# Expert pairs with many tokens: TensorE's code moved behind the program, and a way for up to 64 tokens

## The reference

```python
def hier_moe(x, rg_w, rg_b, re_w, re_b, w_gu, w_down):      # 32 experts, 2 of them per token
    g_p, g_idx = lax.top_k(softmax(t @ rg_w + rg_b), 1)     # one of 4 groups
    e_p, e_idx = lax.top_k(softmax(e_logits), 2)            # two of its 8 experts
    gate = g_p * e_p / sum(e_p)
    ...
    hg, hu = jnp.split(xb @ w_gu[e], 2, axis=-1)            # w_gu: 1024 x 1024 per expert, f32
    y = (jax.nn.silu(hg) * hu) @ w_down[e]                  # w_down: 512 x 1024
    out[token] += gate * y
```

## Time and profile before

| | |
|---|---|
| runs | 2184.54, 2185.58, 2190.74 us; median 2185.58 |
| profiled execution | 2183.85 us, its span 2182.0 us |
| mean granted TensorE clock | 0.92 |
| TensorE matmul busy | 1792.8 us, 82% of the span, 13574 rows |
| VectorE, ScalarE busy | 598.6 us, 394.0 us |
| read from HBM | 535.28 MB |
| instruction queue q8 | 173 packets, 2.83 MB |
| chain that ended last | PE 68%, DMA 19%, issue 5%, DVE 4%, ACT 3% |

### The profile page before, as it was taken

How to read it: one execution, slowest core, us unless ns; L and a number is a source line. 1 busy time by engine, 2 the same in 40 slices (tenths; PEclk the granted TensorE clock), 3 DMA queues, 4 the chain that set the end, 5 groups by cost and what they waited for, 6 DMA issues and landing times.

```text
span 2182.0 us, 30973 instructions
## 1 busy us (share of the span) xinstructions
PE 1792.8 (82%) x13574; PEld 1121.4 (51%) x13574; DVE 598.6 (27%) x1032; ACT 394.0 (18%) x761; POOL 36.0 (2%) x28
## 2 busy tenths in 40 slices
PE   6999999999999987776676778799987677876654
PEld 4788884879886764322222233565984322322211
DVE  1133312123421145321111121574345221211112
ACT  2323201313301133100000001151222000100001
POOL 0000000000000000000000000001030000000000
PEclk9999999999999998888878999899998788988886
DMA  8322333333243523899999998123004899999995
GB/s 336 99 92 97 135 135 142 146 78 130 83 155 135 212 112 129 369 424 425 424 425 425 426 402 318 66 77 117 4 23 182 375 424 425 418 425 425 426 424 225
DMA packets 51468, 539.56 MB, mean 247 GB/s; under 512 B 7441, under 2 KB 16273, under 8 KB 18225
## 3 DMA queue, kind: packets, MB, share of 16 engines
q1 hardware_dynamic: 49248, 527.06, 59.2%
q0 software_dynamic: 1152, 6.29, 0.8%
q10 hardware_dynamic: 848, 3.00, 0.4%
HBM read 535.28 MB, written 1.05 MB: 246 GB/s over the span
## 4 chain that ended last, share of the span: by engine, by line
PE 68%; DMA 19%; issue 5%; DVE 4%; ACT 3%; DVEq 0%; ACTq 0%
PE ps L410 53%; PE ps L417 13%; DMA arena<-in_moe_w_gu 7%; DMA arena<-in_moe_w_down 7%; DMA ring<-in_moe_w_down 3%; PE ps L423 3%; DMA ring<-in_moe_w_gu 1%; DVE x L1371 1%; ACT arena L2172 1%; DVE arena L1360 1%; ACT hb L2168 1%; DVE mT L1947 0%; ACT arena L2443 0%; DVE mT L1950 0%; ACT L2168 0%
## 5 line engine op out<-in xcount | busy, mean ns | idle before, releaser
L410 PE MATMUL ps<-hT,ring 128*128 128x256 f32 (+2 forms) x1888 | 392.0, 372 | 0.0
L410 PEld LDWEIGHTS ps<-hT,ring 128*128 128x128 f32 (+2 forms) x1888 | 330.5, 184 | 53.8 <-issue 3.4
L417 PE MATMUL ps<-arena 128*32 128x512 f32 (+1 forms) x1572 | 243.5, 706 | 107.5 <-issue 68.1
L417 PE MATMUL ps<-ring,arena 128*32 128x512 f32 x1472 | 211.0, 707 | 99.3 <-issue 73.3
L2172 ACT ACTIVATE arena<-ps 128x512 f32<-128x512 f32 (+4 forms) x145 | 94.5, 652 | 888.5 <-PE ps L417 519.8
L410 PE MATMUL ps<-arena 64*64 64x64 f32 (+10 forms) x1944 | 186.6, 324 | 58.8 <-ACT arena L2443 22.2
L417 PEld LDWEIGHTS ps<-arena 128*32 128x32 f32 (+1 forms) x1572 | 63.9, 130 | 264.0 <-issue 204.8
L1360 DVE TENSOR_TENSOR arena<-arena,ps 128x256 f32<-128x256 f32 (+2 forms) x82 | 46.0, 561 | 551.2 <-ACT arena L2168 464.2
L410 PEld LDWEIGHTS ps<-arena 64*64 64x64 f32 (+4 forms) x1944 | 113.2, 159 | 132.5 <-issue 54.0
L417 PEld LDWEIGHTS ps<-ring,arena 128*32 128x32 f32 x1472 | 53.7, 125 | 238.4 <-issue 196.2
L410 PE MATMUL ps<-ring,hT 128*128 128x256 f32 (+4 forms) x576 | 150.1, 419 | 8.7 <-ACT hT L2168 7.0
(11 more groups left out here) (174 smaller groups left out, 1258.8 us busy)
## 6 DMA issues: line engine op xcount, KB each, us to landing
ring<-in_moe_w_gu SPq DMA_DIRECT2D x64, 2048.0 KB, 27.7
arena<-in_moe_w_gu SPq DMA_DIRECT2D x64, 2048.0 KB, 30.9
arena<-in_moe_w_down SPq DMA_DIRECT2D x32, 2048.0 KB, 32.1
ring<-in_moe_w_down SPq DMA_DIRECT2D x32, 2048.0 KB, 31.8
ring<-in_w_merge SPq DMA_DIRECT2D x16, 2048.0 KB, 7.3
ring<-in_w_in SPq DMA_DIRECT2D x10, 2048.0 KB, 7.5
ring<-in_attn_w_qkv SPq DMA_DIRECT2D x6, 2048.0 KB, 7.4
ring<-in_rw_w_rkv SPq DMA_DIRECT2D x6, 2048.0 KB, 7.4
```

Source lines behind the costliest of these rows:

```text
L410: i = t.matmul(o, l, r, start=first, stop=last, skip_group_check=True)
L417: i = t.matmul(o, l, r, start=first, stop=last, skip_group_check=True)
```

## The change

Three things are done.

First, in TensorE's program each pair now has only the common way in place, right behind a compare-and-branch. The rare ways of all 32 pairs are written at the very end of the program, behind the last stage (`rare`, called through `rest`). A pair that goes a rare way branches there and, at its end, branches back to the place behind its common way (`over`). At the beginning of each rare way an instruction (BRANCH_PREFETCH_HINT) announces the branch at its end.

Second, there is a new way with two rounds for 33 to 64 tokens, names with `m2`; that with three is now `m3`. The functions `several(pr, before, R)` write both on all three engines. In the two-round way the gather has 64 columns instead of 128 per row.

Third, a flag `flag3` (over 64 tokens) is worked out by two more VectorE operations and loaded on the rare ways. On VectorE and ScalarE the code stays in place: within the branch for over 32 tokens and not over 96 there is one branch more, with the three-round way first.

The parts of the diff that count (moved code left out):

```diff
@@ tensor_program, moe
+        def several(pr, before, R):
...
+            t.wait_ge(*dve(N + W + "places"))
+            t.wait_ge(*act(N + "all in"))
+            w2 = 2 * CAP * (R - 1)
+            for half in range(2):
+                mm([(psum[1][:, k * P:k * P + w2], x[:, i, k * P:(k + 1) * P], e.oh2[:, i * P:i * P + w2], i == 0, i == 1)
+                    for k in range(4 * half, 4 * half + 4) for i in range(NT)], N + W + f"tokens{half}")
...
+        def rare(pr, before, origin):
+
+            N = M + f"{pr} "
+            with t.bass.body(N + "rare", parent=origin, valid_engines=[t.engine]):
+                more = t.value_load(e.flag3[0:1, pr:pr + 1], min_val=0, max_val=1)
+                t.br_ne(more, 0, N + "more", N + "two")
+                with t.bass.body(N + "two", valid_engines=[t.engine]):
+                    back = t.mark_branch_hint_location()
+                    several(pr, before, 2)
+                    t.br(N + "over").branch_hint(back)
+                with t.bass.body(N + "more", valid_engines=[t.engine]):
+                    most = t.value_load(e.flag2[0:1, pr:pr + 1], min_val=0, max_val=1)
+                    t.br_ne(most, 0, N + "any", N + "three")
+                    with t.bass.body(N + "three", valid_engines=[t.engine]):
+                        back = t.mark_branch_hint_location()
+                        several(pr, before, 3)
+                        t.br(N + "over").branch_hint(back)
...
-            many = t.value_load(e.flag[0:1, pr:pr + 1], min_val=0, max_val=1)
-            with t.If(many != 0):
-                most = t.value_load(e.flag2[0:1, pr:pr + 1], min_val=0, max_val=1)
-                with t.If(most != 0):
...
+            starts.append((pe.n, t.bass.cur_bb))
...
+            t.br_ne(many, 0, N + "rare", N + "common")
+            with t.bass.body(N + "common", valid_engines=[t.engine]):
+                up_to_cap(pr, pe.n)
+                t.br(N + "over")
+            t.bass.switch_bb(N + "over")
...
+        def rest():
+            end = pe.n
+            for pr, (before, origin) in enumerate(starts):
+                rare(pr, before, origin)
+            pe.n = end
...
-    moe(0)
+    rare0 = moe(0)
     rwkv()
-    moe(1)
+    rare1 = moe(1)
+
+    rare0()
+    rare1()
@@ vector_program, moe
             cp(e.flag2, cnt2)
+            ts(cnt2, cnt, 2 * CAP + 0.5, None, ALU.is_gt, None)
+            cp(e.flag3, cnt2)
...
                 with v.Else():
+                    more = v.value_load(e.flag3[0:1, pr:pr + 1], min_val=0, max_val=1)
+                    with v.If(more != 0):
+                        several(pr, before, 3)
+                    with v.Else():
+                        several(pr, before, 2)
```

More of the change, by code:

```diff
@@ L135, with bass @@
     tensor_reduce = reciprocal = tensor_copy = memset = tensor_tensor_scan = dma_start = take
-    then_inc = wait_ge = value_load = If = Else = take
+    then_inc = wait_ge = value_load = If = Else = br = br_ne = body = cur_bb = switch_bb = mark_branch_hint_location = branch_hint = take
+    engine = None
+    @property
+    def bass(self):
+        return self
     def __ne__(self, other):
@@ L345, in memory @@
     e.gates, e.sel, e.pos = (carve(64).rearrange("p (t n) -> p t n", t=NT) for _ in range(3))
-    e.flag, e.flag2 = (carve(16).bitcast(mybir.dt.int32) for _ in range(2))
+    e.flag, e.flag2, e.flag3 = (carve(16).bitcast(mybir.dt.int32) for _ in range(3))
     e.pad = carve(1)
@@ new lines, in any_number @@
+        def any_number(pr, before):
+            N, N0, N1 = M + f"{pr} ", M + f"{pr - 1} ", M + f"{pr + 1} "
+            wg, wd = [N + f"gu{q}" for q in range(4)], [N + f"dn{q}" for q in range(2)]
+            gv, dv = ([wcols(m.w(w), 2, 2 * D) for w in ws] for ws in (wg, wd))
+            pe.n = before
+            t.wait_ge(*dve(N + "all in"))
+            t.wait_ge(*act(N + "all in"))
+            for w in wg:
+                t.wait_ge(*m.w.landed(w))
+            for a in range(2):
+                bufs = (psum[0], psum[1]) if a else (pg, pt)
+                lst = [(dst[:, n * 256:(n + 1) * 256], gv[k // 2][:, k % 2, a * D + c * 512 + n * P:a * D + c * 512 + (n + 1) * P],
+                        hT[:, k, :], k == 0, k == KT - 1)
+                       for c, dst in enumerate(bufs) for n in range(4) for k in range(KT)]
+                if a:
+                    mm_to(lst, before + 14, N + "gu3")
+                else:
+                    mm(lst, N + "f gu0")
+            t.wait_ge(*dve(N + "f hid0"))
+            next_four(pr, pg, N + "f ")
+            for w in wd:
+                t.wait_ge(*m.w.landed(w))
+            t.wait_ge(*dve(N + "f hid1"))
+            for a in range(2):
+                h3 = e.hid[a].rearrange("p (k s) -> p k s", k=4)
+                if a:
+                    t.wait_ge(*act(N1 + "all in"))
+                    t.wait_ge(*dve(N + "f xe"))
+                for i in range(NT):
+                    buf = (pg, pt)[i] if a else psum[i]
+                    lst = [(buf[:, n * 512:(n + 1) * 512], h3[:, k, i * P:(i + 1) * P],
+                            dv[k // 2][:, k % 2, a * D + n * 512:a * D + (n + 1) * 512], k == 0, k == 3)
+                           for n in range(2) for k in range(4)]
+                    if a and i:
+                        mm_to(lst, before + 44, N + "out")
+                    else:
+                        mm(lst, N + f"f down{a}{i}")
+            t.wait_ge(*dve(N1 + "all in"))
@@ new lines, in rare @@
+        def rare(pr, before, origin):
[14 more added lines that the diff above has]
+                        t.br(N + "over").branch_hint(back)
+                    with t.bass.body(N + "any", valid_engines=[t.engine]):
+                        back = t.mark_branch_hint_location()
+                        any_number(pr, before)
+                        t.br(N + "over").branch_hint(back)
@@ L899, in moe @@
         gates_T(psum[1][:, 0:512], M + "first gatesT")
+        starts = []
         for pr in range(E // 2):
[L902 to L905, removed]
+            N = M + f"{pr} "
+            starts.append((pe.n, t.bass.cur_bb))
             if pr == 0:
```

380 lines of the change are left out of this document (183 added, 197 removed).

## The result

The changed kernel takes 2154.50 us (median of four runs, 2152.69 to 2154.96) beside 2185.77 for the kernel before on the same chip: a ratio of 0.9851, 95% interval 0.9834 to 0.9868. I had predicted 2154.6. Timed once more on another chip it took 2152.70 (2152.01 to 2156.66), ratio 0.9847 (0.9834 to 0.9861). The profiled execution took 2154.79, its span is 2153.0, 29.0 less than before. The sum came out; several of its terms did not, and what I took for the price of the way back from a rare pair was something else.

The account below looks back on a forecast made before the run. The weight stream bounds the middle of both expert stages; TensorE decides at each stage's beginning and the first's end. Gains of 24.0 in stage 0 and 5.3 in stage 1 make 29.3: 2183.85 to 2154.6 us, range 2148 to 2161.

Parts of the forecast that it names:

- Stage 0: First expert stage: 24.0 us gained, from 1.4 at pair 12's start, 4.7 and 4.9 ways back, 13.0 in pair 14.
- pair 11 over sooner: Stage 0, end of pair 11: 6.4 us earlier (1220.3 to 1213.9), from earlier stream and less instruction traffic.
- entry of pair 12: Stage 0: three loads and two far jumps ahead of pair 12, 11.0 us, bounds 7 and 14.7; 6.02 before.
- pair 12 itself: Stage 0, three-round pair 12: its own 47.8 us stay.
- way back from it, fetch and clock: Stage 0, behind pairs 12 and 14: announced branch leaves about 0.5 us idle, clock stays up; gains 4.7 and 4.9.
- pair 14, one round less: Stage 0, pair 14: two rounds instead of three gain 13.0 us, bounds 11.5 and 14.
- Start and middle: Stage 0: stream 5.4 us earlier through pair 0's earlier first slot, plus 1.0 from less instruction traffic.
- Rival 1: Ways back from pairs 12 and 14: announcement does nothing, 9.6 us less gain, 2164.2; chance 0.25.
- Stage 1: Second expert stage: 5.3 us gained, 4.1 at pair 0's start and 1.2 from instruction traffic; the rest is stream.
- The likeliest case: Whole kernel: the forecast itself, 2154.6 us, own range 2148 to 2161; chance 0.58.
- Rival 2: Every taken branch restarts the fetch, also at a common pair's end; pair 13 pays 3.7 us: 2158.3; chance 0.08.
- Rival 3: Far code behind the program is dear: five jumps at f us each, passing 2190 from f = 8.9; chance 0.04.

Follow-up runs that it names:

- the early announcement: Changed kernel plus, in every common way, a hint naming the next pair's branch to its rare code: 2148.71, ratio 0.9848; timed again 2151.53 beside 2152.70.
- both announcements: Changed kernel with the next pair's branch to rare code and its second branch, to the three-round code, both announced a pair ahead: 2151.58, ratio 0.9853.

## Why the prediction was right, step by step

Stage 0 was to give 24.0 us and gave 24.4 (1369.25 less 1344.86). Its terms, from the starts in the earlier trace rows and in the rows above, rounded one by one:

| term of the sum | predicted | measured |
|---|---|---|
| pair 11 over sooner | 6.4 | 4.4 |
| entry of pair 12 | -5.0 | -7.3 |
| pair 12 itself | 0 | +2.4 |
| way back from it, fetch and clock | 4.7 | 5.2 |
| pair 13 and entry of pair 14 | 0 | 0.4 |
| pair 14, one round less | 13.0 | 14.0 |
| way back from it, fetch and clock | 4.9 | 5.4 |
| sum | 24.0 | 24.4 |

The table keeps the forecast's names; what its two rows "way back" hold is explained below.

**Start and middle.** Right in mechanism. I took 1.0 us for load and branch and said that no row prices TensorE's branch; there is one, 0.10 us at 883.19. At the beginning both lie within the 0.69, in the stream they hide behind the DMA (0.31 ahead of pair 3 at 945.17, released by the DMA). The slot is 6.6 us sooner, 1.2 of them from ahead of the branch, which leaves the 5.4 forecast. One reading was too short: the "some 360 matmuls" are the three-round way alone; a common pair jumped over the way for any number too, some 550 in all by the kernel's loops. The DMA lost 5.3 us less, and the down chunk of pair 3 starts 5.5 us sooner (976.03 to 970.52). The added 1.0 for instruction traffic isn't there: by pair 11's last down chunk the gain is 4.4 (1215.62 to 1211.23). Fewer packets did not make the stream faster; why it gives 1.1 back I can't say. Skipped code doesn't come whole either: with one way more to skip, the kernel with all ways in place moves 174 packets, the one before 173.

**Entry of pair 12.** The term was mis-sized: 11.0 predicted, 13.31 to 13.84 measured in six kernels without the early announcement. The far jump alone is right (5.8 into pair 14); the second one adds 7.5 to 8.5, not 3.7 and a load of 1.2. I priced it by the gaps after rare pairs, 3.54 and 3.67, and these are jumps of 6.77 and 6.91 us of which half was covered. The branch rows give the price whole: 6.04 and 6.82 us at pair 12, of which only 1.3 lies under pair 11's last matmuls (1214.60 to 1215.91), and nothing runs that could cover the second.

**Pair 12 itself** gave 2.4 that I had at 0: 45.5 us for 47.8. A stop of 1.30 us inside it, ahead of 1232.13 before, is gone, and its first rows ran at a higher clock. These 2.4 and the -2.3 of the entry cancel; so do 2.0 too few at the start and 2.4 more in the last four terms of the table. The total is nearer than its parts deserve.

**Ways back.** The size was right (0 instead of my 0.5), the cause was not. The step took 3.54 and 3.67 us for the fetch of an unannounced jump back and said "if the announced branch finds its target there". Both halves fail. The jump back took 0.3 us before the change too, and with no announcement it takes 0.3 to 0.4; the gaps were pair 13's and pair 15's own jumps over their rare ways, which the common way in line takes away whatever is announced. So the 9.6 us of these two terms belong to the same mechanism as the 5 us ahead of the other pairs, and that they came out as forecast is luck in the reasoning. Rival 1 set the time at 2164.2 for an announcement that does nothing. It does nothing for the time here, and the time is 2154.5 all the same: the rival shared the wrong reading.

The Trainium skill, Runtime: NRT & Kernel Launch, Instruction fetch mechanics, has the instruction memory as two lines of 16 KiB, with no cache that gains from locality, so that a taken branch out of the two pages must fetch; the same section gives TensorE 128 KiB, which is 2048 instructions. By the two lines the way back without the announcement should have cost what every far jump costs. The measured 0.3 to 0.4 us speak against that for TensorE, while the jumps into the rare code, 5.9 to 7.2 us, agree. Pair 12's 376 matmuls with a weight load each are some 750 instructions, an estimate; they would fit into 128 KiB.

**Pair 14.** 14.0 for 13.0; by the run without the two-round way the third round is 13.2. The narrower gather took 3.79 for 3.84: nothing, as said.

**Pair 15 and the floor.** No DMA wait shows up in pairs 13 to 15, as forecast. With the early announcement the last row of stage 0 starts at 1338.03 and 1339.31, with both at 1335.66, where the kernel with common ways alone has 1339.46.

**Between the stages** I had 0; it gave 1.7 (at stage 1's routing matmuls the kernel is 26.1 ahead, 1695.98 less 1669.88). The same kernel differs by more from one execution to the next (last section), so this is no effect of the change that I could show.

**Stage 1.** 5.3 predicted. Pair 0's first slot is issued at 1682.83, 29.8 us sooner, so the beginning gave 3.7 for the 4.1 I had; 4.0 stand at the last down chunk. The 1.2 for instruction traffic isn't there, as in stage 0. The last eight rows then ran at the lower clock (1.92 for four rows, 1.02 before) and took 1.1 back. So 2.9 net; with the 1.7 from between the stages the total is 29.0 for 29.3.

**The chances.** The likeliest case held as to time. Rival 2, that every taken branch restarts the fetch, is excluded by the ways back: they are taken and cost 0.3 us. The branch at the end of a common pair, to the next instruction, has no row in the trace but at the last pair, and there is no idle time at its place (0 between pairs in stage 0, 0.31 for a DMA). Rival 3 counted five far fetches; three were dear (6.0 to 6.8 us each, not 8.9), and the two ways back were none.

## What to carry to other kernels

A taken branch to code that is not at hand costs TensorE some 6 us here, near or far, and leaves about 5 us of idle time ahead of each pair, since the queue reaches it 1.3 us before the matmuls run out. What counts is how many such branches stand on the path, not how much code they cross. Put the way that nearly always runs in line, the rare one far away, and see that the rare one is reached by a single jump: a second branch behind it cost 7.5 to 8.5 us, more than half a round. The return needs no announcement; the way out profits from one given a pair ahead, as long as TensorE and not the stream decides there. And before a gap ahead of a pair is put down to the jump that ended the last one, look at the rows of the branches: they tell which branch took the time.

## What the runs showed of the hardware

- A taken branch of TensorE to code not at hand took 5.0 to 7.7 us before the change, with a median of 6.1 (L911), over some 550 matmuls by the kernel's loops, and 6.2 to 6.4 over some 180 (L913); to the end of the program it took 5.9 to 6.6 and over some 820 matmuls 4.7 to 7.2. One that isn't taken took 0.06 to 0.10.
- The way back took 0.3 us in place, over some 130 matmuls of the common code, in all three cases of the kernel before; in the kernel with all ways in place 0.31 and, once, 2.22. Over the two-round code besides it took 6.05. From the end of the program it took 0.3 to 0.4 us, with and without an announcement, in every kernel. How much code TensorE has at hand was not measured.
- The announcement of a conditional branch, given before the flag is loaded, cut the idle time ahead of pair 14 from 5.80 to 0.26 us and left a stop of 2.75 us 16 rows later, so 2.8 us net. A second one in the same place had no effect.
- The stage between the mixtures, whose code no kernel changes, took (from pair 15's first row of the way back to the tokens to stage 1's routing matmuls) 327.7 us before, 326.0 and 326.5 after (two executions), 333.5 with all ways in place, 324.3 with common ways alone, 330.8 with both announcements, and 323.8 and 326.3 in two executions of the kernel with the early one. TensorE's idle time put down to "issue" in it was, in this order, 12.0, 9.1, 9.8, 14.3, 8.7, 12.4, 8.7 and 11.1 us. It is made of stops like this one, of the kernel with all ways in place:

```profile
1502.25 2.61 PE L415 MATMUL ps<-arena 64*64 64x64 f32 x84 [3.69 <-issue]
```

  These are waits for instructions: in the eight traces named, every such stop over 0.3 us ends 2.2 to 3.0 us after a packet of the instruction queue has started (here 1499.81), while these packets mostly come every 3.5 to 4 us in this stage of short matmuls. There are 37 or 38 of them in every kernel. Why the stops add up to more in one execution than in another stays open; one and the same kernel differs by 2.5 us, so where the code lies can't be all of it. I did not foresee it.
